# Expert blocks of 128 rows instead of 64-row pairs in a two-layer mixer and MoE kernel

## The reference

```python
def hier_moe(h, w_rg, b_rg, w_re, b_re, w_gate, w_up, w_down):
    ...
    top_v, top_i = lax.top_k(e_logits, TOP_K)                 # two experts per token
    e_w = jax.nn.softmax(top_v, axis=-1) * g_w[:, None]
    expert_id = g_sel[:, None] * EXPERTS_PER_GROUP + top_i.astype(jnp.int32)
    ...
    def expert_block(args):                                    # rows of one expert
        xb, e = args
        hid = jax.nn.silu(xb @ w_gate[e]) * (xb @ w_up[e])     # 1024 -> 256, twice
        return hid @ w_down[e]                                 # 256 -> 1024
    ...
    out = jnp.zeros((T, D), jnp.float32).at[tok_pad].add(y.astype(jnp.float32) * w_pad[:, None])

h_lat = h_lat + g2 * hier_moe(...)                             # g2: a gate per feature
return rmsnorm(h_lat, norm_final)
```

## Time and profile before

| | us |
|---|---|
| median of three runs | 3016.74 |
| the profiled execution | 3026.95 |
| its span | 3025.0 |
| PE busy | 2745.6 (91%) |
| DVE busy | 1469.1 (49%) |
| POOL busy | 722.0 (24%) |
| ACT busy | 506.7 (17%) |

### The profile page before, as it was taken

How to read it: one execution, slowest core, us unless ns; L and a number is a source line. 1 busy time by engine, 2 the same in 40 slices (tenths; PEclk the granted TensorE clock), 3 DMA queues, 4 the chain that set the end, 5 groups by cost and what they waited for, 6 DMA issues and landing times. The chain is left out here.

```text
span 3025.0 us, 28672 instructions
## 1 busy us (share of the span) xinstructions
PE 2745.6 (91%) x10136; PEld 1553.2 (51%) x10136; DVE 1469.1 (49%) x3286; ACT 506.7 (17%) x1087; POOL 722.0 (24%) x620
## 2 busy tenths in 40 slices
PE   6999999999998599978979996999989889988888
PEld 3445634446444333324435656888879743333333
DVE  1134401203012322212236459989889987777773
ACT  2033300011001011122026411111122200000004
POOL 0000000000000022210000006654566555555540
PEclk8999999999998699988989898999989989999998
DMA  5101161530212699961210208999999789999982
GB/s 214 56 28 39 68 271 64 198 125 8 83 65 106 261 389 398 392 255 50 84 63 15 93 20 298 400 403 409 415 370 415 266 343 413 414 412 413 413 349 116
DMA packets 142576, 695.23 MB, mean 230 GB/s; under 512 B 20466, under 2 KB 21874, under 8 KB 110578
## 3 DMA queue, kind: packets, MB, share of 16 engines
q1 hardware_dynamic: 59858, 409.35, 34.1%
q0 software_dynamic: 81792, 281.07, 23.9%
q10 hardware_dynamic: 800, 3.15, 0.3%
HBM read 702.93 MB, written 48.23 MB: 248 GB/s over the span
## 5 line engine op out<-in xcount | busy, mean ns | idle before, releaser
L513 PE MATMUL ps<-hT,pm_coef_table 128*128 128x256 f32 (+1 forms) x2432 | 507.4, 371 | 30.4 <-DVE hT L439 24.4
L2537 PE MATMUL ps<-hT 128*128 128x512 f32 x1024 | 457.9, 602 | 50.7 <-DMA hT<-in_peer_v 29.4
L2390 POOL DMA_INDIRECT wring<-in_peer_u,pm_rows x256 | 336.9, 1316 | 683.9 <-DVEq L2759 463.0
L513 PEld LDWEIGHTS ps<-hT,pm_coef_table 128*128 128x128 f32 x2432 | 444.5, 192 | 87.5 <-issue 25.1
L513 PE MATMUL ps<-hT,wring 128*128 128x512 f32 (+2 forms) x976 | 412.2, 583 | 10.4 <-PEq L678 2.8
L2390 POOL DMA_INDIRECT wring<-in_peer_v,pm_rows x256 | 319.4, 1248 | 246.0 <-DVE h_tok L2810 207.1
L2810 DVE SCALAR_TENSOR_TENSOR h_tok<-wring,pm_coef,h_tok 128x1024 f32<-128x1024 f32 x256 | 324.3, 1281 | 106.3 <-DMA wring<-in_peer_v,pm_rows 105.0
L2537 PEld LDWEIGHTS ps<-hT 128*128 128x128 f32 x1024 | 190.4, 191 | 317.6 <-issue 226.7
L2643 DVE CUSTOM_DVE_ANT_0 wring<-wring,pm_coef_table 128x1024 f32<-128x1024 f32 x256 | 303.2, 1217 | 40.2 <-DMA wring<-in_peer_u,pm_rows 39.6
L513 PEld LDWEIGHTS ps<-hT,wring 128*128 128x128 f32 (+1 forms) x976 | 185.1, 191 | 231.6 <-issue 229.8
L1579 POOL COPY ex_idx<-row_token 128x1 uint32 (+1 forms) x24 | 4.4, 183 | 1153.7 <-PEq L1711 1021.3
(11 more groups left out here) (429 smaller groups left out, 2711.5 us busy)
## 6 DMA issues: line engine op xcount, KB each, us to landing
ex_gu<-in_experts SPq DMA_DIRECT2D x32, 2048.0 KB, 12.9
pm_coef_table<-in_peer_uT SPq DMA_DIRECT2D x64, 1024.0 KB, 8.1
hT<-in_peer_v SPq DMA_DIRECT2D x64, 1024.0 KB, 8.0
ex_dn<-in_experts SPq DMA_DIRECT2D x48, 1024.0 KB
wring<-in_w_in SPq DMA_DIRECT2D x21, 2048.0 KB, 8.2
wring<-in_experts SPq DMA_DIRECT2D x16, 2048.0 KB
ada_w<-in_w_ada SPq DMA_DIRECT2D x12, 2048.0 KB, 11.5
g_dram_out<-pm_coef_table SPq DMA_DIRECT2D x64, 256.0 KB, 9.4
```

The source lines that it names most:

```text
L513: mm = env.nc.tensor.matmul(out, w[:, k, lo:hi], rhs(k), start=(k == 0), stop=(k == KD - 1))
L2390: nc.gpsimd.indirect_dma_start(ring[n % RING], None, dram[name], bass.IndirectOffsetOnAxis(ap=rows[:, t, j:j + 1], axis=0)).then_inc(got[n ...
L2537: mm = nc.tensor.matmul(env.ps[:, OUT[k], :], W[n % 2][:, at:at + P], vr[p % 2][:, m % 2 * D + k % 2 * WBLK:m % 2 * D + (k % 2 + 1) * WBLK ...
```

## The change

The expert blocks become 128 rows high (`EB` = 128). There are 32 fixed blocks, one for each expert, and 7 overflow blocks, 39 in all, and each is a full PE pass of its own: no pairs. The blocks are run in the order of `ORDER`, which puts an overflow block behind every fourth expert from the sixth on. The loops are written out (unrolled) on all engines. The weight rings are kept in single blocks: 6 slots of `gu`, 4 of `dn`; 6 `gu` and 4 `dn` blocks are now loaded during the router. There are 4 buffers for fetched rows and 3 for results, which take 12 KB a partition that POOL clears once during the router. POOL no longer copies row numbers. The features are split: 4 on DVE, 4 on ACT. The results are copied out of PSUM by DVE, which multiplies by the gate (`env.gates[:, 1]`) in the same instruction. The scatter goes to row pick x 512 + token, so `y_dram` has 1024 rows, each of which is written; the 12 MB write is gone, and the sum stage loads each token tile's two picks with one plain transfer on SP. There DVE needs two instructions for each tile, and ACT's scaling is gone.

The diff, cut to its core; most lines taken out are left away here, since they stand in the listing above:

```diff
-                nc.sync.dma_start(dram["y_dram"].rearrange("(b p) d -> p b d", p=P),
-                                  env.gates[:, 0, :].unsqueeze(1).broadcast_to([P, NB, D])).then_inc(env.y_set, 16)
...
-EB = P // 2
-LATER = (PICKS * S - PICKS) // EB + 1
-NEB = NE + LATER
-NB = NEB // 2
+EB = P
+LATER = (PICKS * S - 1) // EB
+NB = NE + LATER
 SLOT = 2
-LAST = NB // SLOT
-TRIPLES = LATER // 2
-GUS = 3
-ROUND = 6
+GUS = 6
+DNS = 4
+XS, YS = 4, 3
+ORDER = []
+for _e in range(NE):
+    ORDER.append(_e)
+    if _e >= 5 and _e % 4 == 1:
+        ORDER.append(NE + (_e - 5) // 4)
...
+                for b in range(GUS):
+                    nc.sync.dma_start(E.gu[b], dram["experts"][ORDER[b], :, 0:GUW]).then_inc(E.gu_got[b], 16)
+                    if b < DNS:
+                        nc.sync.dma_start(E.dn[b], dram["experts"][ORDER[b], :, GUW:]).then_inc(E.dn_got[b], 16)
...
+                V.tensor_copy(in_pair[:], env.ps[:, t_rows[0], 0:NB]).then_inc(env.bank_free[t_rows[0]], 1)
                 evacuated(env, v, t_rows)
+                step(v, [V.tensor_scalar(unused[:], in_pair[:], 0.0, UNUSED, ALU.is_equal, ALU.mult),
+                         V.tensor_scalar(second[:], in_pair[:], float(S), -float(S), ALU.is_gt, ALU.mult)])
+                step(v, [V.scalar_tensor_tensor(E.row_place[:], in_pair[:], -1.0, unused[:], ALU.add, ALU.add),
+                         V.tensor_tensor(second[:], second[:], unused[:], ALU.add)])
+                step(v, [V.scalar_tensor_tensor(E.row_token[:], in_pair[:], -1.0, second[:], ALU.add, ALU.add)])
...
+                def gather(b):
+                    if b >= XS:
+                        pool.wait_ge(rows_full, 2 * (b - XS) + 2)
+                    nc.gpsimd.indirect_dma_start(x[b % XS], None, dram["xn_dram"], bass.IndirectOffsetOnAxis(
+                        ap=E.row_token[:, ORDER[b]:ORDER[b] + 1], axis=0), bounds_check=S - 1,
+                        oob_is_err=False).then_inc(x_got[b % XS], 16)
+
+                def scatter(b):
+                    pool.wait_ge(y_done, 2 * b + 2)
+                    nc.gpsimd.indirect_dma_start(dram["y_dram"], bass.IndirectOffsetOnAxis(
+                        ap=E.row_place[:, ORDER[b]:ORDER[b] + 1], axis=0), y[b % YS], None,
+                        bounds_check=PICKS * S - 1, oob_is_err=False).then_inc(y_out[b % YS], 16)
+
+                for b in range(XS + 2):
+                    gather(b)
+                for b in range(NB):
+                    if b + XS + 2 < NB:
+                        gather(b + XS + 2)
+                    scatter(b)
...
+                def load(to, b, lo, hi, got):
+
+                    if ORDER[b] < NE:
+                        nc.sync.dma_start(to, dram["experts"][ORDER[b], :, lo:hi]).then_inc(got, 16)
+                        return
+                    n = ORDER[b] - NE
+                    expert = nc.sync.value_load(E.block_expert[0:1, n:n + 1], min_val=0, max_val=NE - 1)
+                    used = nc.sync.value_load(E.later_used[0:1, n:n + 1], min_val=0, max_val=1)
+                    nc.sync.dma_start(to, dram["experts"][bass.ds(expert, 1), :, lo:hi].rearrange("o p n -> p (o n)"),
+                                      cond=used).then_inc(got, 16)
+
+                def down(b):
+                    if b >= DNS:
+                        sp.wait_ge(dn_full, 2 * (b - DNS) + 2)
+                        load(E.dn[b % DNS], b, GUW, GUW + EFT * D, dn_got[b % DNS])
...
-                def gate_up(i, n):
-                    b, s = ROUND * i + n, n % SLOT
-                    pe.wait_ge(gu_got[n % GUS], 32 * (ROUND // GUS * i + n // GUS) + 32)
-                    pe.wait_ge(xT_done, KD * b + KD)
+                def gate_up(b):
+                    s = b % SLOT
+                    pe.wait_ge(gu_got[b % GUS], 16 * (b // GUS + 1))
                     for k in range(KD):
-                        for h, r in enumerate(rows_of):
-                            mm = nc.tensor.matmul(env.ps[r, GU[s], :], xT[:, s, k, r], wg[n % GUS][h][:, k, :],
-                                                  start=(k == 0), stop=(k == KD - 1))
+                        if k % HALF_K == 0:
+                            pe.wait_ge((xT_low, xT_high)[k // HALF_K], b + 1)
+                        mm = nc.tensor.matmul(env.ps[:, GU[s], :], xT[:, s, k, :], wg[b % GUS][:, k, :],
+                                              start=(k == 0), stop=(k == KD - 1))
                     mm.then_inc(gu_full, 1)
...
-                    pe.wait_ge(dn_got[s], 32 * (ROUND // SLOT * i + n // SLOT) + 32)
+                def down(b):
+                    s = b % SLOT
+                    pe.wait_ge(dn_got[b % DNS], 16 * (b // DNS + 1))
                     pe.wait_ge(hidT_done, b + 1)
                     for q in range(2):
-                        pe.wait_ge(y_done, 2 * b + q + 1)
+                        if b:
+                            pe.wait_ge(y_done, 2 * b + q - 1)
                         for k in range(EFT):
-                            for h, r in enumerate(rows_of):
-                                mm = nc.tensor.matmul(env.ps[r, DOWN[q], :], hidT[:, s, k, r],
-                                                      wd[s][h][:, k, q * WBLK:(q + 1) * WBLK],
-                                                      start=(k == 0), stop=(k == EFT - 1))
+                            mm = nc.tensor.matmul(env.ps[:, DOWN[q], :], hidT[:, s, k, :],
+                                                  wd[b % DNS][:, k, q * WBLK:(q + 1) * WBLK],
+                                                  start=(k == 0), stop=(k == EFT - 1))
                         mm.then_inc(dn_full, 1)
...
+                rows(0)
+                gate_up(0)
+                rows(1)
+                for b in range(NB):
+                    if b + 1 < NB:
+                        gate_up(b + 1)
+                    hidden(b)
+                    if b + 2 < NB:
+                        rows(b + 2)
+                    down(b)
...
-                    if not first:
-                        act.wait_ge(y_out[s], 16 * i)
-                    for n in range(2):
-                        act.wait_ge(dn_full, 2 * b + n + 1)
-                        nc.scalar.activation(y[:, s, n * WBLK:(n + 1) * WBLK], env.ps[:, DOWN[n], :],
-                                             ACT.Copy).then_inc(y_done, 1)
...
+                def high_features(b):
+                    act.wait_ge(rows_full, 2 * b + 2)
+                    for j in range(HALF_K):
+                        k = HALF_K + j
+                        ins = nc.scalar.activation(xT[:, b % SLOT, k, :], env.ps[:, ROWS[1], j * P:(j + 1) * P],
+                                                   ACT.Identity, scale=gain(k), bias=shift(k))
+                    ins.then_inc(xT_high, 1)
+
+                high_features(0)
+                gate(0)
+                high_features(1)
+                for b in range(NB):
+                    if b + 1 < NB:
+                        gate(b + 1)
+                    turned(b)
+                    if b + 2 < NB:
+                        high_features(b + 2)
...
+                def low_features(b):
+                    v.wait_ge(rows_full, 2 * b + 1)
+                    for k in range(HALF_K):
+                        ins = nc.vector.tensor_scalar(xT[:, b % SLOT, k, :], env.ps[:, ROWS[0], k * P:(k + 1) * P],
+                                                      gain(k), shift(k), ALU.mult, ALU.add)
+                    ins.then_inc(xT_low, 1)
...
+                def gated(b):
+                    if b >= YS:
+                        v.wait_ge(y_out[b % YS], 16 * (b // YS))
+                    for q in range(2):
+                        cs = slice(q * WBLK, (q + 1) * WBLK)
+                        v.wait_ge(dn_full, 2 * b + q + 1)
+                        nc.vector.tensor_tensor(y[b % YS][:, cs], env.gates[:, 1, cs], env.ps[:, DOWN[q], :],
+                                                ALU.mult).then_inc(y_done, 1)
+                low_features(0)
+                low_features(1)
+                product(0)
+                for b in range(NB):
+                    if b + 1 < NB:
+                        product(b + 1)
+                    if b + 2 < NB:
+                        low_features(b + 2)
+                    gated(b)
...
+                picked = dram["y_dram"].rearrange("(k t p) d -> t p k d", k=PICKS, p=P)
+                nc.sync.dma_start(y[:, 0], picked[0]).then_inc(got[0], 16)
+                for t in range(1, NT):
+                    nc.sync.dma_start(y[:, t], picked[t]).then_inc(got[t], 16)
...
-            @block.gpsimd
-            def _(pool):
...
-                        nc.gpsimd.indirect_dma_start(y[:, t, k, :], None, dram["y_dram"], bass.IndirectOffsetOnAxis(
-                            ap=E.pos[:, k, t:t + 1], axis=0)).then_inc(got[t], 16)
...
-                def first(t):
-                    act.wait_ge(got[t], 16 * PICKS)
```

(19 more changed lines are left out.)

289 lines of the change are left out of this document (65 added, 224 removed).

## The result

The changed kernel takes **3168.58 us** (3166.63 to 3168.74, 4 runs), the kernel before 3017.14 us in the same series (3012.98 to 3019.17): ratio 1.050, 95% interval [1.0485, 1.0514]. That is +151.4 us; forecast were +147.4 and 3164 us.

A forecast was written before the change was run, and what follows sets the result against it. PE was taken to bound the expert stage, with transfers just keeping up. Terms 167.7 - 1.1 - 8.0 - 2.5 - 1.2 - 7.5 = +147.4 us on the 3016.74 median gave 3164 us; range 3150 to 3192.

The forecast's parts named there:

- The turn: Expert stage on PE: 39 full-width turns of 11.5 us replace 24 of 11.70, +167.7 us (bounds +165.4 to +175.5).
- I take 11.5: Cost in us of one new PE turn, chosen between 11.44 from the full-width rows and the old turn's 11.70.
- Rival 1: Expert matmuls: a full-width one costs no more than a narrow one, 0.218 us a record; 2965 us, faster; 3%.
- rival 2: Expert stage: the transfers set it, so its time stays; 2996 us, faster; 1%.
- rival 3: Expert turns: late hidden or gated copies make PE wait 1 us in every block, +39; 3203 us; 6%.
- rival 4: Expert stage: unused overflow blocks cost nothing, so fewer turns run; 3083 us; 1%.
- Weights, fill: Expert stage: PE's waits for weights go, -1.1 us; first two gate_ups wait less for features, -2.5 us (0 to -4).
- four on DVE ... and four on ACT: Fill: sharing the features between two engines takes a little more than half of the 4.3 us waits off, -2.5 us.
- Entry: Router to first expert rows: first fetch lands 6.8 us sooner, POOL's copy and gap go; -8.0 us (-1.2 to -9).
- Exit: Way out of the expert stage: the last scatter loses its copy, -1.2 us.
- Sum: Sum stage: first root 5.2 us earlier, tiles 2 and 3 -1.16 each; PE's next stage -7.5 us (0 to -10).
- The write, the loops: The 12 MB write, over which PE ran without a gap, and the jumps removed by unrolling: 0 us each.

The follow-up runs named there:

- Experiment 3: Changed kernel with every gate, up and down matmul taking 64 of the 128 rows, alone, nothing in the other half of the columns: 3174.58 us, ratio 1.0503.
- experiment 2: Changed kernel without its seven overflow blocks, which are empty for these inputs: 3083.91 us, ratio 1.0207 to the kernel before.
- Experiment 7: Changed kernel with all 8 feature tiles of a block scaled and shifted on DVE, none on ACT: 3174.09 us, ratio 1.0492 to the kernel before.
- Experiment 10: Kernel before with PE waiting for four feature tiles ahead of gate_up and four in its middle, not all eight ahead: 3015.3 us, ratio 0.9992.
- experiment 6: Changed kernel with only 3 gate/up and 2 down weight tiles loaded ahead, the others issued by SP at the expert stage's start: 3179.37 us.
- experiment 4: Changed kernel in all its parts but with 24 pairs of 64-row blocks as before: 3003.08 us, ratio 0.9929 to the kernel before.
- experiment 5: Changed kernel repeated as it is, in another series: 3172.86 us, ratio 1.0489, +147.8 us to the kernel before of that series.
- experiment 1: Kernel before with results scattered by pick and token and the 12 MB write gone, nothing else changed: 3018.75 us, ratio 0.9994.
- Experiment 8: Changed kernel with the sum's rows fetched by 8 indirect transfers from POOL, not plain ones from SP: 3172.61 us, ratio 1.0493 to the kernel before.
- Experiment 9: Kernel before with only the sum's arithmetic changed: one weighted DVE instruction per pick, no ACT scaling, expert gate left out: 3010.85 us, ratio 0.9974.

## Why the prediction was right, step by step

**The turn: right, and a little dear.** The price of a full-width matmul, 0.429 us a record whatever its rows, held (6.87 / 16 = 0.429), and so did the count of 39 turns without a branch. 39 x 11.39 - 24 x 11.69 = +163.6 us stand against +167.7. The overestimate is the step "I take 11.5": the rows of full width gave 11.44, the measured turn is 11.39, since the hidden transposes, taken at 0.28 from the mixed turn, are 0.22 among full-width work. So the trace's own bound from the full-width rows was the better number. Experiment 3 sizes the difference that is left out in it: 0.30 us per turn for the changes of width. The Trainium skill (TensorEngine Tiling (Array Packing), Key Properties) says that a change of tiling mode drains TensorE; these traces agree. Rival 1 is refuted by the turn, rival 2 by the DMA share of 0.65 and by PE's turns without a wait for weights, rival 3 by the turns without idle brackets (the longest behind the first is 11.47, the second), rival 4 by the 39 turns and by experiment 2.

**Weights, fill.** Last down minus first rows grew by 159.4; less the 163.6 of the turns that leaves -4.2, forecast -3.6 (1.1 + 2.5). PE's waits in the fill gave 2.45 of it (1.97 + 2.29 against 0.70 + 1.11), the first gate_up at the low clock 0.4 (10.05 against 9.67), and the 1.1 us of waits for weights are gone. The size was right, the mechanism half wrong: "four on DVE ... and four on ACT" is not what gains. Experiments 7 and 10 give it to the split wait, which the prediction had read over in the diff.

**Entry: right, 1.4 too much.** From issue to use the first fetch takes 4.0 us where it took 9.9, so 5.9 of the 6.6 us; experiment 6, which puts 8 MB of weights beside it again (5 MB before the change), brings 10.2 back. The forecast had 6.8 there, as it took the shortest landing, 3.1 us, for the whole way to PE. The copy's end (1.2) gave 0.8: POOL issues 43.97 us behind the router's start instead of 44.73.

**Exit: wrong sign.** "The last scatter loses its copy: -1.2" was read to the issue of the scatter and no further; +3.2 came. The stage ends when POOL's queue is drained, and this is longer with more transfers behind it. With 48 indirect transfers in the stage (before, experiment 4) it takes 3.98 and 3.99 us, with 64 (experiment 2) 5.29, with 78 (changed kernel, experiments 3 and 5) 6.44: 0.082 us for each one more, over both steps. Experiment 2 differs from the changed kernel in nothing but the number of blocks, so it goes with their number; each block is one fetch and one scatter, and the runs don't separate the two. It does not go with the stage's length: in experiment 3 the stage is 11.4 us longer and the drain still 6.44. Nor is 0.082 us a price for other stages: the drain of the sum stage before takes 16.44 us with 8 such transfers; it begins while they are still being issued. The 1.1 us between the last issue and the drain have no experiment made for them. The places are a part: with the old ones this stretch is 3.4 to 3.6 us in four profiles, with the new ones and the same 24 pairs 4.1 (experiment 1) and 3.8 (4), with the blocks of 128 rows 4.2 to 4.7. The first matmul of the stage behind the sum lies 50.0 us behind the last scatter's issue instead of 55.6: 5.5 nearer, where the prediction's sign said 7.

**Sum: right, 1.5 too little.** The first root on ACT, behind the fourth projection copy at 1499.64:

```profile
1502.58 0.29 ACT L1792 ACTIVATE es_rs<-es_ss,eps 128x1 f32<-128x1 f32 x1
```

From start to start this is 2.94 us, 5.5 less than before (1359.38 - 1350.96 = 8.42), forecast 5.2. The forecast's 2.9 was meant from end to end, which came out as 2.63 (1502.87 - 1500.24). ACT's scaling was what held DVE back. From that root to the next stage's first matmul it is 20.20 us instead of 23.24, so 3.0 less where the forecast had two tiles' 1.16 each; another 0.4 lies ahead of the copies. Experiments 8 and 9 give all of the 9 us to the arithmetic, ACT's scaling and DVE's third instruction taken together.

**The write, the loops: 0, and 0** (experiments 1 and 4). The prediction makes of the Trainium skill's rule a stall at each of PE's jumps, which is more than it says: it speaks of a branch out of the fetched window. Whether a jump of PE leaves that window no run here shows, so 11.69 us a turn with and without loops neither bears the rule out nor refutes it.

**The whole.** The errors were -4.1 (turns), -0.6 (fill and waits), +1.4 (entry), +4.4 (exit), -1.5 (sum), -0.4 together: the stretches sum to +147.0 against +147.4 forecast. That closeness is partly luck, as two errors of four microseconds cancel. The other 4 us to the median's +151.4 are not traced. They are within what the untouched stretches vary between profiles (the router's start 970.98 to 978.22, the rest 1638.28 to 1647.56), and the series of experiment 5 gave +147.8.

## What to carry to other kernels

Price a matmul by the columns that stream through and by whether a second one can run beside it in the other half of the array, not by its rows: two half-width matmuls side by side cost as much as one full one (6.97 against 6.87 us for a gate_up here), so filling the array with rows that may be empty gains nothing, and every block more costs a turn. When a change bundles several edits, sum it stretch by stretch and look for the parts with the other sign: here the edits around the blocks were worth 0.7% by themselves (ratio 0.993), and the blocks cost 5.7% on top (1.050 / 0.993). Follow a stage to the instruction at which all engines meet, the drains too, not to its last useful one.

## What the hardware showed that I had not expected

- POOL's drain at the end of the expert stage grew by 0.082 us for each indirect transfer that the stage had issued (3.98, 5.29, 6.44 us for 48, 64, 78), although the last of them had landed, with every other engine waiting for it.
- PE pays 0.30 us a turn for going between 128*64 and 128*128 work and back: 11.69 against 11.39 us with the same matmuls otherwise, all of it in the first two records behind each change.
- A fetch of 128 rows that takes 4.0 us from issue to use by itself takes 10.2 us with 8 MB of plain transfers issued beside it.
- Moving the wait for half of the features into the middle of gate_up was worth as much as a second engine's help was thought to be: with four of eight features on either engine, or all on one, gate_up started 2.67 us behind the transposes.
